# One masked decay matrix per head, both scan directions in one exponent, in the chunked state-space scan of a two-block transformer kernel

## What is computed

```python
a = (dt * A); a_cs = jnp.cumsum(a, axis=-1)          # per chunk and head, forward; the backward scan runs on flipped data
seg = a_cs[..., :, None] - a_cs[..., None, :]
Lm = jnp.exp(jnp.where(lower, seg, -jnp.inf))        # 128 x 128 decay of one head in one chunk
cb = jnp.einsum('bclgn,bcsgn->bcgls', Cc, Bc)        # one 128 x 128 product per chunk and group
y_diag = jnp.einsum('bcgls,bcgrls,bcsgrp->bclgrp', cb, Lm, x)      # x = xs * dt
y_off = jnp.einsum('bclgn,bcgrpn,bcgrl->bclgrp', Cc, h_prev, jnp.exp(a_cs))
...
return y_f + flip(y_b) + d_skip[:, None] * xs
```

## Time and profile before

| | us |
|---|---|
| median of 3 runs | 4062.03 |
| lowest, highest | 4055.98, 4067.8 |
| the profiled execution | 4055.48 |
| its span, first to last instruction | 4053.7 |
| TensorE busy in it | 3684.6 |
| VectorE, ScalarE, GpSimd busy | 1207.0, 725.1, 491.8 |

### The profile page before, as it was taken

One profiled execution on the slowest core, in us unless ns is written; L12 is line 12 of the kernel. 1 busy time (PEld: TensorE's weight loads), 2 busy tenths in 40 slices (PEclk: granted clock), 3 DMA queues, 4 the chain that ended last, 5 costly groups with the idle time before them and its releaser, 6 DMA issues.

```text
span 4053.7 us, 33521 instructions
## 1 busy us (share of the span) xinstructions
PE 3684.6 (91%) x12856; PEld 1789.4 (44%) x12856; DVE 1207.0 (30%) x2815; ACT 725.1 (18%) x1560; POOL 491.8 (12%) x437
## 2 busy tenths in 40 slices
PE   6899898899999978888888888899999999999999
PEld 3355554444444433332333334455444445454444
DVE  2336555634310130211101114443221134432211
ACT  2023333222310110000000003322110123221100
POOL 1003234411100000000000002100221011012210
PEclk8899898899999989999999999999999999999999
DMA  8322223212212459999999992102222130032220
GB/s 252 125 76 74 73 63 94 71 47 58 81 62 83 184 217 409 409 409 409 409 409 409 409 401 92 37 27 83 81 65 78 48 103 32 21 97 75 83 68 36
DMA packets 302156, 634.12 MB, mean 156 GB/s; under 512 B 32499, under 2 KB 145763, under 8 KB 301743
## 3 DMA queue, kind: packets, MB, share of 16 engines
q1 hardware_dynamic: 240480, 591.96, 39.3%
q10 hardware_dynamic: 61519, 40.02, 3.5%
HBM read 625.50 MB, written 10.24 MB: 157 GB/s over the span
## 4 chain that ended last, share of the span: by engine, by line
PE 51%; DMA 18%; DVE 3%; ACT 1%; issue 1%; POOL 0%; SPq 0%; DVEq 0%; ACTq 0%
PE psum L295 26%; DMA arena<-in_w_exp_up_dram 7%; DMA arena<-in_w_exp_gate_dram 7%; PE psum L1496 6%; DMA arena<-in_w_exp_down_dram 4%; PE psum L2764 4%; PE psum L2728 4%; PE psum L2269 3%; PE psum L1324 2%; PE psum L1352 1%; PE psum L2749 1%; PE psum L2218 1%; PE psum L1333 1%; PE psum L2187 1%; PE psum L2659 1%
## 5 line engine op out<-in xcount | busy, mean ns | idle before, releaser
L295 PE MATMUL psum<-arena 128*128 128x512 f32 (+1 forms) x3200 | 1299.4, 564 | 4.5 <-POOL arena L1887 2.4
L295 PEld LDWEIGHTS psum<-arena 128*128 128x128 f32 x3200 | 608.5, 192 | 681.5 <-issue 658.8
L2269 PE MATMUL psum<-arena 128*64 128x512 f32 x3072 | 695.1, 597 | 150.6 <-DMA arena<-in_w_exp_up_dram 77.5
L2269 PEld LDWEIGHTS psum<-arena 128*64 128x64 f32 x3072 | 233.6, 136 | 593.3 <-issue 572.8
L1496 PE MATMUL psum<-arena 128*128 128x512 f32 x768 | 349.4, 609 | 0.0
L715 PE MATMUL psum<-arena 128*128 128x512 f32 (+1 forms) x768 | 269.8, 511 | 1.3 <-ACT arena L538 1.3
L1496 PEld LDWEIGHTS psum<-arena 128*128 128x128 f32 x768 | 146.2, 194 | 189.3 <-issue 188.4
L1430 DVE CUSTOM_DVE_ANT_0 arena<-psum,arena 128x512 f32<-128x512 f32 (+3 forms) x224 | 114.0, 546 | 386.9 <-PE psum L1324 379.0
L2807 POOL TENSOR_SCALAR arena<-arena 128x512 f32<-128x512 f32 x88 | 138.6, 1576 | 701.1 <-ACT arena L2786 701.1
L715 PEld LDWEIGHTS psum<-arena 128*128 128x128 f32 x768 | 150.9, 199 | 124.5 <-issue 113.8
L2813 DVE SCALAR_TENSOR_TENSOR arena<-arena 128x512 f32<-128x512 f32 x88 | 66.2, 752 | 426.6 <-POOL arena L2807 426.6
(11 more groups left out here) (270 smaller groups left out, 3146.9 us busy)
## 6 DMA issues: line engine op xcount, KB each, us to landing
arena<-in_w_exp_gate_dram SPq DMA_DIRECT2D x128, 1024.0 KB, 18.9
arena<-in_w_exp_up_dram SPq DMA_DIRECT2D x128, 1024.0 KB, 18.6
arena<-in_w_exp_down_dram SPq DMA_DIRECT2D x128, 1024.0 KB, 18.6
arena<-in_w_in_dram SPq DMA_DIRECT2D x64, 1024.0 KB, 5.3
arena<-in_w_up_dram SPq DMA_DIRECT2D x88, 512.0 KB, 4.9
arena<-in_w_ada_dram SPq DMA_DIRECT2D x24, 1024.0 KB, 8.1
arena<-in_w_down_dram SPq DMA_DIRECT2D x20, 1024.0 KB, 5.0
arena<-acs_scratch ACTq DMA_DIRECT2D x64, 256.0 KB, 3.5
```

Of the source, the lines that this page charges most:

```text
L295: mm = pe.matmul(shaped(b, l, r), l, r, start=kt == 0, stop=kt == nkt - 1)
L2269: mm = pe.matmul(banks[n][64 * j:64 * j + 64, :], lhs[:, kt, 64 * j:64 * j + 64], w, start=kt == 0, stop=kt == 2 * nkb - 1)
```

## The change

For each item there is now one matrix for both directions. The two clipped differences become two masked ones: `late` is 0 for source tokens up to and including the target and -1e30 otherwise, `early` the opposite without the diagonal; VectorE forms (row - column) + mask for each direction with one scalar_tensor_tensor per head, and takes the maximum of both (a new 128 x 512 instruction). The column is now the cumulative sum less log(dt), so the exponent contains dt, and x*dt is not formed any more. The diagonal belongs to both directions; its backward part, CB's diagonal times dt, is added to the skip weight (`skip`, with a reduction of CB against the identity). ScalarE takes one exponent per item (L1123 of the new file), GpSimd multiplies all items with the unmasked CB (L1285 of the new file), and TensorE forms one product per head straight from `xs2` (L1074). ScalarE issues both next row loads ahead of the exponent; the load of `RB[0]` waits for the forward differences, that of `RB[1]` for the maximum (it holds the backward differences). Three `ER` buffers rotate in place of four. In the dt stage come four small mask instructions, a clip, one logarithm and one subtraction. `yTb` has two buffers. Group 3 is woven at 0.57, with two empty steps between its last item and its norm, on all engines.

```diff
-        yTb = bufs(1, 512)[0]
+        yTb = bufs(2, 512)
         RB = bufs(2, 512)
-        ER = bufs(4, 512)
+        ER = bufs(3, 512)
...
+            act.wait_ge(*at("dtmin"))
+            act.activation(lnd, lnd, ACT.Ln, bias=0.0, scale=1.0).then_inc(*up(S("act_dt"), ("lnd",)))
...
+            dve.tensor_scalar(lnd, dt[:, 0:256], 1e-37, None, ALU.max).then_inc(*up(v, ("dtmin",)))
+            dve.tensor_tensor(early, con("uge"), ident, ALU.subtract).then_inc(*up(v))
+            dve.tensor_scalar(late, con("ule"), 1.0, -NEG, ALU.subtract, ALU.mult).then_inc(*up(v))
+            dve.wait_ge(*now(v))
+            dve.tensor_scalar(early, early, 1.0, -NEG, ALU.subtract, ALU.mult).then_inc(*up(v))
...
+            dve.tensor_tensor(acs[:, 0:256], acs[:, 0:256], lnd, ALU.subtract).then_inc(*up(v, ("aclog",)))
...
-            for d in range(2):
-                pe.wait_ge(*at("M", g, n, d))
-                if hq == 0:
-                    pe.wait_ge(*at("xd", u + d))
+            pe.wait_ge(*at("M", g, n))
             for h in range(4):
                 hh = 4 * hq + h
-                for d in range(2):
-                    mm = pe.matmul(y[:, hh * 64:hh * 64 + 64], r3(ER[(2 * n + d) % 4], 128)[:, h, :], xd_of(u + d)[:, hh * 64:hh * 64 + 64],
-                                   start=d == 0, stop=d == 1)
+                mm = pe.matmul(y[:, hh * 64:hh * 64 + 64], r3(ER[n_of(g, n) % 3], 128)[:, h, :], xs2[g % 2][:, c, hh * 64:hh * 64 + 64], start=True, stop=True)
...
+            if n_of(g, n):
+                act.wait_ge(*at("seg", g - (n < 1), n - 1 if n else 7, d))
...
+                    e = ER[n_of(g, n) % 3]
                     for d in range(2):
-                        k = 2 * n + d
-                        act.wait_ge(*at("seg", g, k))
...
-                        act.activation(ER[k % 4], RB[k % 2], ACT.Exp, bias=0.0, scale=1.0).then_inc(*up(S("act_er"), ("er", g, k)))
-                        load_rows(act, g, k + 2)
+                        load_rows(act, g, n + 1, d)
+                    act.wait_ge(*at("seg", g, n, 1))
+                    act.activation(e, e, ACT.Exp, bias=0.0, scale=1.0).then_inc(*up(S("act_er"), ("er", g, n)))
...
             if g == 3:
+                yield from idle(2)
                 act_rstd(act, ("ssd", g), ssy, 4)
                 act_finish(act, g)
...
-                if 4 * g + i:
-                    act.wait_ge(*at("yD", 4 * g + i - 1))
...
+                if t > 1:
+                    act.wait_ge(*at("yD", t - 2))
...
-                dve.tensor_tensor(cb[:, 0:128], PS.of(key)[:, 0:128], con("ule"), ALU.mult).then_inc(*up(S("dve_cb")))
-                dve.tensor_tensor(cb[:, 128:256], PS.of(key)[:, 0:128], con("uge"), ALU.mult).then_inc(*up(S("dve_cb"), ("free", key), ("cbt", g, c)))
-            for d in range(2):
+                dve.tensor_copy(cb, PS.of(key)[:, 0:128]).then_inc(*up(S("dve_cb"), ("cbt", g, c)))
+                dve.tensor_tensor_reduce(out=cjunk, in0=PS.of(key)[:, 0:128], in1=ident, scale=1.0, scalar=0.0, op0=ALU.mult, op1=ALU.add,
+                                         accum_out=cbd[:, c % 2:c % 2 + 1]).then_inc(*up(S("dve_cb"), ("free", key)))
+                dve.wait_ge(*now(S("dve_cb")))
+                dve.scalar_tensor_tensor(out=skip[c % 2], in0=r3(dt, 64)[:, c, 32 + 8 * g:40 + 8 * g], scalar=cbd[:, c % 2:c % 2 + 1],
+                                         in1=dsk[:, 8 * g:8 * g + 8], op0=ALU.mult, op1=ALU.add).then_inc(*up(S("dve_cb"), ("skip", g, c)))
...
+            for d, (dst, mask) in enumerate(((e, late), (RB[1], early))):
                 h0 = 8 * g + 4 * hq
...
                 for h in range(4):
                     col = ac3[:, c, 32 * d + h0 + h:32 * d + h0 + h + 1]
-                    r_ = rb[:, h * 128:(h + 1) * 128]
-                    keys = [("seg", g, 2 * n + d)] if h == 3 else []
-                    dve.tensor_scalar(r_, r_, col, 0.0, ALU.subtract, ALU.min).then_inc(*up(S("dve_seg"), *keys))
-                if d:
-                    eb = r3(ER[(2 * n + d) % 4], 128)
-                    dve.wait_ge(*at("er", g, 2 * n + d))
-                    dve.tensor_tensor(eb, eb, rep(cb[:, 128:256], 4), ALU.mult).then_inc(*up(S("dve_M"), ("M", g, n, d)))
+                    one_head = slice(h * 128, h * 128 + 128)
+                    keys = [("seg", g, n, 0)] if d == 0 and h == 3 else []
+                    dve.scalar_tensor_tensor(out=dst[:, one_head], in0=RB[d][:, one_head], scalar=col, in1=mask, op0=ALU.subtract, op1=ALU.add).then_inc(
+                        *up(v, *keys))
+            dve.wait_ge(*now(v))
+            dve.tensor_tensor(e, e, RB[1], ALU.max).then_inc(*up(v, ("seg", g, n, 1)))
...
-            weave(main, chain(pe_na_qk(pe, 0, PG), pe_na_qk(pe, 1, PG)), 0.65)
+            weave(main, chain(pe_na_qk(pe, 0, PG), pe_na_qk(pe, 1, PG)), 0.57)
```

132 lines of the change are left out of this document (66 added, 66 removed).

## The result

The changed kernel took 4070.83 us (median of 11 runs, 4062.3 to 4076.38), the kernel before, measured beside it, 4055.98 (11 runs, 4048.49 to 4067.8). The ratio is 1.0031, 95% interval 1.0017 to 1.0044: 13 us slower by the ratio, 15 by the medians. Forecast were 4071.0, and that the change is about neutral.

The account below looks back on a forecast made before the run. Bound: a chain of VectorE, ScalarE and GpSimd in the chunks that TensorE waits for. Groups 0 to 2 +10.8, group 3 -1.5, dt stage +0.4 give +9.7, from 4055.5 to 4065; median 6.5 above the profiled execution: 4071, range 4042 to 4092.

Parts of the forecast that it names:

- TensorE's 34.6 us: Half of the y products' 69.2 us leaves TensorE; a gain only if TensorE's queue is the bound.
- The chain of two items: From VectorE's maximum through load issue, table load, exponent and GpSimd: 17.6 us per two items, +8.1 over groups 0 to 2.
- Tail to item 7: Behind a group's last L1233, item 7 is ready after 6.4 us instead of 4.83: +1.55 in each of three groups.
- y of item 7 becomes half, -1.0 in each of three groups: On TensorE behind a group's last wait: y of item 7, 1.97 us, is halved, -3.0 in the sum.
- Groups 0 to 2, +10.8: Two-item chains +8.1, tails to item 7 +4.7, first halves +1.0, halved y of item 7 -3.0.
- Group 3, -1.5: Norm wait 8.1 instead of 13.2 us (-5.1), about +4.5 of waiting for items, second yTb frees a bank.
- Sum +9.7: Groups 0 to 2, group 3 and the dt stage together, from 4055.5 of the profiled execution to 4065.
- The +0.4 of the dt stage: The subtraction ahead of the first weighing in the dt stage costs about 0.4 us.
- the stretch behind the chunks changes by more than 3 us: A sign set beforehand that the prediction is wrong: a change that large in the 592 us behind the chunks.
- TensorE's queue: Rival, faster: TensorE's own list decides, so half of the 34.6 and the norm's 5.1 come through, 4040; chance 0.18.
- Load and switch hidden after all: Rival: table load runs ahead of the wait or rows land in 3 us; -12 over six cycles, 4059; chance 0.15.
- Collision: Rival, slower: VectorE's new differences are held beside GpSimd's product, +19 over four groups, 4090; chance 0.17.

Follow-up runs that it names:

- before_half_y: The kernel before with only the forward y product of each head, the backward half of y left out; ratio 0.9987 to the kernel before.
- after_table: The changed kernel with a one-column exponent ahead of each item's row loads, so the table switch runs during VectorE's maximum; ratio 1.0015 to the kernel before.
- after_rb3: The changed kernel with a third row buffer for the backward direction and a single yTb; ratio 1.0008 to the kernel before.
- after_oldweave: The changed kernel with group 3's weave weight back at 0.65 and no two empty steps before its norm; ratio 1.0035 to the kernel before.
- before_stt: The kernel before with its 256 differences done by the three-operand instruction instead of the two-operand one; ratio 1.0007 to the kernel before.

## Why the prediction was right, and where it was not

**TensorE's 34.6 us are worth next to nothing:** right, shown by before_half_y. The y products' busy time went from 69.2 to 39.5. The prediction let all of it turn into waiting; in the trace idle time grew by 25 us and TensorE's other work by 11, at a lower granted clock (0.89 instead of 0.92). The prediction had no term for that.

**The chain of two items:** right in size. Predicted 17.6 for a pair, 35.2 for two; measured 35.17, 35.69 and 35.55 in groups 0, 1 and 2. The single pairs are 18.2 to 18.8 and 16.9, so the sum of two was met better than either. In the first pair of group 1 the time from maximum to maximum is 6.45 instead of the 4.91 of the sum, because VectorE waits 2.62 us for TensorE's CB product (L1056), which stood behind a projection and a y: there the chain passes through TensorE's queue, which the sum had left out. In the second pair, shown above, the steps are: L1256 and L1259 1.33 (1.35), odd item's differences 2.23 (2.24), maximum 0.69 (0.75), from there to the even item's maximum 4.62 (3.75 + 1.16), maximum 0.69, issue and table load 1.73 (0.45 + 1.28), exponent 0.77 (0.65), GpSimd's four 4.87 (5.20). The exposed table load was shown by after_table. Its place was named rightly; that the issue ahead of it can't go before the maximum either was in the sum, but not seen as a term that can be removed by itself (after_rb3, 9 us).

**Tail to item 7:** predicted 6.4, measured 549.58 - 543.20 = 6.38 in group 1, and the same in groups 0 and 2. **"y of item 7 becomes half, -1.0 in each of three groups"** came in two of them and failed in the one it was read from: in group 0 it went from 2.91 to 1.97 us, in group 2 from 2.40 to 1.13, in group 1 it stayed at 1.97. The timeline of TensorE there, against the earlier trace rows:

```profile
549.58 1.97 PE L1074 MATMUL psum<-arena 128*128 128x64 f32 x8 [4.04 <-POOL arena L1285]
551.34 3.27 PE L1081 MATMUL psum<-arena 128*128 128x512 f32 x4
```

Eight instructions took the 1.97 us that sixteen had taken at a granted clock of 1.00. The wait ahead is 4.04 instead of 2.01 us. The windows around the eight at 514.00, which took 1.00 us and which TensorE met straight from other work, and around these (us, busy of PE, PEld, DVE, ACT, POOL, clock, DMA share, GB/s):

```profile
512.00:516.50 4.50, 4.20 (x24) 2.81 (x23) 1.84 (x8) 3.79 (x4) 1.26 (x1) 1.00 0.30 83
...
549.50:554.50 5.00, 4.92 (x13) 3.13 (x14) 0.69 (x1) 0.53 (x1) 1.02 (x2) 0.55 0.01 3
```

The granted clock is 1.00 there and 0.55 here, almost all at the lower of its two levels (1.2 of 2.4 GHz). So the half of group 1 gave nothing.

**Groups 0 to 2, +10.8:** against the first profiles +12.9 (390.0 against 377.1 us from the state copy of group 0, at 305.2 and 305.3, to that of group 3). By the stages above it is +9.0 in the first two pairs (predicted +8.1), +2.4 in the first halves (+1.0), +1.5 in the rest of the groups (+4.7 - 3.0 = +1.7). Against the second profile of before, 368.6 us, it is +21.4, of it +14.4 in the pairs. What is weak is the base: "33.64, 29.76 and 34.01" are one execution with several collisions; in the second they are 31.72, 30.42 and 29.88. The trace showed the sets of 2.77 beside those of 0.88, and I used them only for a rival of the new kernel, not as a doubt about the old one.

**Group 3, -1.5:** measured -6.0 by the first profiles, -2.4 by the second. The norm's 13.2 to 8.1 was exact (8.00). In after_oldweave the norm wait is 5.2 longer and the wait for items 8.6 shorter, so waits for items do pay it back, as the +4.5 of the sum said; how much in time is open.

**Sum +9.7:** the times say 13 to 15 us. The +0.4 of the dt stage did not show: group 0 starts at 305.2 instead of 305.3. That the forecast of 4071 met 4070.83 owes something to luck: the median of three that I started from, 4062.03, was 6 us above the 4055.98 of eleven runs, and the sum was 5 us too small; the two cancel.

**The falsifier** "the stretch behind the chunks changes by more than 3 us" fired by 6.2 us and was a bad one: that stretch has a spread of 14 us of its own.

**The rivals.** TensorE's queue: refuted as what sets the time, though it holds the chain once in a first pair, as above. Load and switch hidden after all: refuted for the changed kernel, and after_table and after_rb3 show what they would have given. Its price of 12 us was about right at the norm turn for the table, and each is worth 6 to 9 in the times, both together 14. Collision: seven of the 32 sets of eight in the first profile after were busy for 2.5 to 3.2 us instead of 2.2; the whole of it is 75.0 us against 32 x 2.19 = 70.1, so 5 us of VectorE's time, not 19. The rule of the Trainium skill named in the prediction (GPSIMD Engine Reference, section Key points) holds in kind: the new ones stay exposed, by the 5 us. The Trainium skill (ScalarE: Activation LUTs, section What ACT_TABLE_LOAD costs) adds a drain of 1.38 us to each switch. No profile here shows it: the exponent above began 1.30 us behind the start of its table load.

## What to carry to other kernels

Work taken from an engine that waits for the others mostly lengthens its wait, and on TensorE part of it came back here as a lower granted clock. Before fusing two half-items into one, ask what the halves did under each other: here one exponent for two directions made every engine's list shorter, and put all differences, the maximum, a DMA issue and a table load in series. The gains of two edits in one chain need not add: here they overlapped in the pairs of items. A queue's small instructions that wait for nothing themselves (a table load, a DMA issue) cost their full time once they stand behind a wait; a dummy activation ahead of the wait, or a further buffer, buys it back. And look at two profiles of the kernel before, before its stalls are taken for its pace.

## What was not expected of the hardware

Four differences on VectorE took 0.88 or 2.77 us according to whether they began 0.62 us ahead of a product on GpSimd or 0.23 us. In the second case two of the four were held, each until 0.08 or 0.09 us behind the end of one GpSimd instruction, and the other two ran at their usual pace, while GpSimd kept its 1.27. The form with two inputs is held too: in before_stt four took 2.94 beside GpSimd, in the changed kernel eight took 2.71 with one GpSimd product in their first 0.6 us.

And fewer matmuls need not be quicker. In the first profile of the changed kernel six sets of eight y products took 1.97 us each at a granted clock of 0.50; TensorE had waited 3.4 to 5.6 us ahead of them. Sets that it met straight from other work took 1.00 at 1.00. The length of the wait alone does not settle it: one set behind 4.40 us took 1.48.
